# A convolution's norm moved in among the last steps of an attention, an SBUF copy issued sooner, and the second token tile split ahead of the last norm

## The reference, cut to what matters

```
for l in range(2):
    y = hybrid_mixer(x)                      # latent attention | convolution, then @ w_o
    x = layer_norm(ALPHA * x + y)            # "mix" norm
    y = memory_cross_attention(x, mem)       # @ w_q, softmax over 256 memory rows, @ w_o
    x = layer_norm(ALPHA * x + y)            # "cross" norm
    y = swiglu_ffn(x)                        # @ w_in, silu(g) * up, @ w_down
    x = layer_norm(ALPHA * x + y)            # "ffn" norm

def hybrid_mixer(x):
    c_q, c_kv, k_r, u = split(x @ w_in + b_in)
    y_att = mla_group(c_q, c_kv, k_r)        # 8 heads, 4 blocks of 128 queries, chunk-causal
    a, g = split(u)
    h = causal_depthwise_conv(a * sigmoid(g))            # 31 taps, 512 channels
    y_conv = silu(layer_norm(h) * cn_g + cn_b)           # norm over the 512 channels
    return concatenate([y_att, y_conv]) @ w_o
```

## Time and profile before

| what | value |
|---|---|
| median of 3 runs | 3571.17 us (3569.41 to 3573.1) |
| the profiled execution's own time | 3575.26 us |
| its span in the trace | 3573.4 us |
| PE busy | 3258.4 us (91%) |
| DVE busy | 1321.7 us (37%) |
| ACT busy | 875.4 us (24%) |
| mean granted TensorE clock | 0.954 of full speed |

### The profile page before, as it was taken

One profiled execution on the slowest core, in us unless ns is written; L12 is line 12 of the kernel. 1 busy time (PEld: TensorE's weight loads), 2 busy tenths in 40 slices (PEclk: granted clock), 3 DMA queues, 4 the chain that ended last, 5 costly groups with the idle time before them and its releaser, 6 DMA issues.

```text
span 3573.4 us, 35777 instructions
## 1 busy us (share of the span) xinstructions
PE 3258.4 (91%) x15128; PEld 2248.8 (63%) x15128; DVE 1321.7 (37%) x2223; ACT 875.4 (24%) x1387; POOL 131.4 (4%) x122
## 2 busy tenths in 40 slices
PE   6998899999998899998999999899699999999994
PEld 5677677877667677876888867677343333433331
DVE  3675443335675443335333444533311111111112
ACT  2342322222342322222233431122111111111111
POOL 0000000001000000001100000000100000000001
PEclk9999999999999999998999999899799999999997
DMA  4122122223112122322211321023599999999996
GB/s 153 59 71 83 59 83 92 97 98 117 59 62 92 59 83 92 103 102 85 74 54 54 94 75 53 33 92 143 209 425 426 426 425 426 426 425 426 426 426 240
DMA packets 229493, 627.62 MB, mean 176 GB/s; under 512 B 14736, under 2 KB 136464, under 8 KB 179920
## 3 DMA queue, kind: packets, MB, share of 16 engines
q1 hardware_dynamic: 207312, 579.37, 41.8%
q10 hardware_dynamic: 19824, 37.77, 3.0%
q0 software_dynamic: 2192, 8.13, 0.8%
HBM read 600.32 MB, written 22.81 MB: 174 GB/s over the span
## 4 chain that ended last, share of the span: by engine, by line
PE 66%; DMA 17%; DVE 10%; ACT 3%; POOL 2%; issue 2%; ACTq 0%; DVEq 0%; POOLq 0%
PE bank L120 64%; DMA piece<-in_moe_w 4%; DMA piece_high<-in_moe_w 3%; DMA mT_slot<-in_moe_w 3%; DMA xT<-in_moe_w 3%; DVE gate_acc L138 2%; PE bank L123 2%; DVE x_tok L138 1%; POOL root L135 1%; DMA memT<-in_moe_w 1%; DMA norm_room<-in_moe_w 1%; DMA y_att_slot<-in_moe_w 1%; DVE stat L153 1%; DVE piece_rounded L135 1%; ACT piece_high_rounded L126 1%
## 5 line engine op out<-in xcount | busy, mean ns | idle before, releaser
L120 PE MATMUL bank<-xT_rounded,piece_high_rounded 128*128 128x512 f32 (+1 forms) x1408 | 554.7, 394 | 25.1 <-DVE xT_low_rounded L135 25.1
L135 DVE TENSOR_TENSOR piece_rounded<-piece,piece_high_rounded 128x2048 fp32r<-128x2048 f32 (+1 forms) x156 | 342.1, 2199 | 575.2 <-ACT piece_high_rounded L126 574.8
L120 PE MATMUL bank<-xT_rounded,piece_rounded 128*128 128x512 f32 (+1 forms) x1408 | 542.1, 385 | 0.0
L120 PE MATMUL bank<-xT_low_rounded,piece_high_rounded 128*128 128x512 f32 (+1 forms) x1408 | 538.2, 382 | 0.0
L135 DVE TENSOR_TENSOR gate_and_hidden<-gate_and_hidden,bank 64x512 f32<-64x512 f32 x64 | 69.2, 1081 | 837.0 <-ACT gate_and_hidden L126 837.0
L126 ACT ACTIVATE piece_high_rounded<-piece 128x2048 fp32r<-128x2048 f32 (+1 forms) x156 | 283.0, 1820 | 287.6 <-DMA piece<-in_ffn_w_down 119.1
L120 PEld LDWEIGHTS bank<-xT_rounded,piece_high_rounded 128*128 128x128 f32 x1408 | 270.2, 192 | 80.9 <-DVE xT_low_rounded L135 26.3
L120 PEld LDWEIGHTS bank<-xT_low_rounded,piece_high_rounded 128*128 128x128 f32 x1408 | 269.9, 192 | 56.0 <-issue 4.4
L120 PEld LDWEIGHTS bank<-xT_rounded,piece_rounded 128*128 128x128 f32 x1408 | 268.4, 191 | 56.5
L120 PE MATMUL bank<-piece,xeT 128*64 128x512 f32 x488 | 239.1, 644 | 18.7 <-DMA piece<-in_moe_w 7.3
L120 PE MATMUL bank<-piece_high,xeT 128*64 128x512 f32 x464 | 185.3, 633 | 14.4 <-DMA piece<-in_moe_w 9.5
(11 more groups left out here) (337 smaller groups left out, 5054.3 us busy)
## 6 DMA issues: line engine op xcount, KB each, us to landing
piece<-in_moe_w SPq DMA_DIRECT2D x90, 1024.0 KB, 16.5
piece_high<-in_moe_w SPq DMA_DIRECT2D x88, 1024.0 KB, 16.5
xT<-in_moe_w SPq DMA_DIRECT2D x59, 1024.0 KB, 16.7
mT_slot<-in_moe_w SPq DMA_DIRECT2D x58, 1024.0 KB, 17.3
piece<-in_ffn_w_in SPq DMA_DIRECT2D x40, 1024.0 KB, 5.0
memT<-in_moe_w SPq DMA_DIRECT2D x30, 1024.0 KB, 15.8
y_att_slot<-in_moe_w SPq DMA_DIRECT2D x30, 1024.0 KB, 16.5
norm_room<-in_moe_w SPq DMA_DIRECT2D x29, 1024.0 KB, 17.0
```

What stands on the lines that cost most here:

```text
L120: return self.engine.matmul(*a, **k) if self.engine is not None else Nothing()
L135: return self.engine.tensor_tensor(*a, **k) if self.engine is not None else Nothing()
```

## The change

1. The convolution's norm. A new `z_turned_pe`, called in steps 28 to 31 of the attention's PE program behind the memory's keys, transposes tile i = n - 28. A new `z_dve`, called at the end of DVE's steps 29 to 32, norms tile n - 29. The result goes to a new tile `z_tok`, which lies where `mem_v_early` is, so `z_dve` also waits for the DMA that moves the memory's values away. `cross_pe` begins with the transposes back, ahead of the output product instead of between its first two groups.
2. That DMA is issued by ACT at the end of its step 23 instead of behind the attention.
3. In every output product with `turned`, tile 1 is transposed between the two pieces of tile 3 (`turned(1)`), and DVE splits tiles 0 and 1 both behind the norm of tile 2, ahead of the add and norm of tile 3. This is in the mix, cross and ffn products of both layers. The merge of the second network calls its `turned` at the old place alone.

```diff
@@ -326,6 +326,8 @@
         carve_from(XT_LOW_AT)
         y_room = carve("yT", CT, S, twin=True)
         self.mem_v_early = carve("mem_v_early", MT, D)
+        carve_from(XT_LOW_AT + CT * S)
+        self.z_tok = carve("z_tok", NT, CONV)
         carve_from(hT_at)
         z_room = carve("zT", CT, S, twin=True)
         self.yT = [y_room[:, k, :] for k in range(CT)] + [z_room[:, k, :] for k in range(CT)]
@@ -722,7 +724,7 @@
             e.also(key, "summed", half, i)
             self.banks.give((key, half, i), key, "added", half, i)
 
-    def project_out_pe(self, e, key, label, kt, lhs, lhs_ready, turned=None, behind_first=None):
+    def project_out_pe(self, e, key, label, kt, lhs, lhs_ready, turned=None):
 
         starts = list(range(0, kt, SLOT // BANK))
         for half in range(2):
@@ -733,8 +735,6 @@
                 for i in range(NT):
                     self.out_tile_pe(e, key, kt, lhs, lhs_ready, half, k0, n, i)
                 self.release(e, n)
-                if behind_first and not half and not k0:
-                    behind_first()
         if turned:
             n0, n1 = self.pe_piece(e, label), self.pe_piece(e, label)
             for tiles in ((0, 1), (2,), (3,)):
@@ -743,6 +743,8 @@
                         self.out_tile_pe(e, key, kt, lhs, lhs_ready, 1, k0, n, i)
                     if tiles[-1] == NT - 1:
                         self.release(e, n)
+                        if k0 == starts[-2]:
+                            turned(1)
                 if tiles == (2,):
                     turned(0)
 
@@ -1039,6 +1041,8 @@
                     self.half_values_pe(e, l, n)
                 else:
                     self.half_keys_pe(e, l, n - 16)
+                if h == HEADS - 1:
+                    self.z_turned_pe(e, l, i)
             if 2 <= n <= len(steps) + 1:
                 h, i = steps[n - 2]
                 bank = banks.take(e, "pT", l, n - 2)
@@ -1061,6 +1065,15 @@
                 ins.then_inc(*e.tick("pe", "y", l, n - 3))
                 if i == NT - 1 and h % 2 == 1:
                     banks.give(("y", l, h // 2), "y_split", l, h // 2)
+
+    def z_turned_pe(self, e, layer, i):
+
+        bank = self.banks.take(e, "zT", layer, i)
+        for c4 in range(CT):
+            e.wait_ge(*self.at("conv", layer, c4, TAPS - 1))
+        self.transposes(e, bank, [self.gate_acc[:, c4, i * P:(i + 1) * P] for c4 in range(CT)]).then_inc(
+            *e.tick("pe", "zT", layer, i))
+        self.banks.give(("zT", layer, i), "z", layer, i)
 
     def half_keys_pe(self, e, layer, u):
 
@@ -1205,6 +1218,11 @@
                     self.values_act(e, l, n // 4, n // 2 % 2)
                 else:
                     self.keys_act(e, l, n // 2 - 8)
+            if n == 23:
+                e.wait_ge(*at("pe", "k", l, HEADS // 2 - 1))
+                for q in range(4):
+                    e.wait_ge(*at("mem_v", l, q, MT - 1))
+                e.dma_start(self.mem_v, self.mem_v_early).then_inc(*e.lands("memory_values_moved", "mem_v_home", l))
 
     def mixer_dve(self, e, layer):
         l, at = layer, self.at
@@ -1282,7 +1300,22 @@
             if n < len(steps) and n % 4 == 0:
                 self.dve_piece(e, "memory values" if n < 16 else "memory keys")
             self.convolve(e, l, taps, 4)
-        self.taps = taps
+            if 0 <= n - len(steps) + 3 < NT:
+                self.z_dve(e, l, n - len(steps) + 3)
+        assert next(taps, None) is None
+
+    def z_dve(self, e, layer, i):
+        bank = self.bank("zT", layer, i)
+        e.wait_ge(*self.at("pe", "zT", layer, i))
+        e.bn_stats(self.stat[:, i, 0, :], bank[:, :]).then_inc(*e.tick())
+        e.wait_ge(*e.own())
+        e.bn_aggr(self.mean_var[:, i, :], self.stat[:, i, 0, :]).then_inc(*e.tick())
+        e.wait_ge(*e.own())
+        self.root_dve(e, i, 1, self.mean_var[:, i, 1:2], 1.0, LN_EPS, "z", layer, i)
+        e.wait_ge(*self.at("root", "z", layer, i))
+        e.wait_ge(*self.at("mem_v_home", layer))
+        e.tensor_scalar(self.z_tok[:, i, :], bank[:, :], self.mean_var[:, i, 0:1], self.root[:, i, 0:1],
+                        ALU.subtract, ALU.mult).then_inc(*e.tick("z", layer, i))
 
     def convolve(self, e, layer, taps, most):
         for _ in range(most):
@@ -1318,28 +1351,18 @@
     def cross_pe(self, e, layer):
         e.begin(f"cross{layer}")
         l, banks, at = layer, self.banks, self.at
-        for i in range(NT):
-            bank = banks.take(e, "zT", l, i)
-            for c4 in range(CT):
-                e.wait_ge(*at("conv", l, c4, TAPS - 1))
-            self.transposes(e, bank, [self.gate_acc[:, c4, i * P:(i + 1) * P] for c4 in range(CT)]).then_inc(
-                *e.tick("pe", "zT", l, i))
-            banks.give(("zT", l, i), "z", l, i)
-        def z_back():
-            for c4 in range(CT):
-                bank = banks.take(e, "zb", l, c4)
-                for i in range(NT):
-                    e.wait_ge(*at("z", l, i))
-                self.transposes(e, bank, [self.v_tok[:, i, c4 * P:(c4 + 1) * P] for i in range(NT)]).then_inc(
-                    *e.tick("pe", "zb", l, c4))
-                banks.give(("zb", l, c4), "silu", l, c4)
-
+        for c4 in range(CT):
+            bank = banks.take(e, "zb", l, c4)
+            for i in range(NT):
+                e.wait_ge(*at("z", l, i))
+            self.transposes(e, bank, [self.z_tok[:, i, c4 * P:(c4 + 1) * P] for i in range(NT)]).then_inc(
+                *e.tick("pe", "zb", l, c4))
+            banks.give(("zb", l, c4), "silu", l, c4)
         self.project_out_pe(e, f"mix{l}", "mix out", KD,
                             lambda k, i: (self.yT[k][:, i * P:(i + 1) * P], self.yT_low[k][:, i * P:(i + 1) * P]),
                             lambda k0: [("z_split" if k0 else "y_split", l, k) for k in range(CT)],
-                            lambda i: self.rows_to_T_pe(e, f"xT_mix{l}", i, self.x_tok, f"mix{l}", "normed", i), z_back)
-        for i in (1, 2):
-            self.rows_to_T_pe(e, f"xT_mix{l}", i, self.x_tok, f"mix{l}", "normed", i)
+                            lambda i: self.rows_to_T_pe(e, f"xT_mix{l}", i, self.x_tok, f"mix{l}", "normed", i))
+        self.rows_to_T_pe(e, f"xT_mix{l}", 2, self.x_tok, f"mix{l}", "normed", 2)
 
         for j in range(KD // 2):
             n = self.pe_piece(e, "cross query")
@@ -1397,8 +1420,7 @@
                             lambda k, i: (self.oT[:, k, i * P:(i + 1) * P], self.oT_low[:, k, i * P:(i + 1) * P]),
                             [("xo_split", l, h, v) for h in range(XH) for v in range(2)],
                             lambda i: self.rows_to_T_pe(e, f"xT_cross{l}", i, self.x_tok, f"cross{l}", "normed", i))
-        for i in (1, 2):
-            self.rows_to_T_pe(e, f"xT_cross{l}", i, self.x_tok, f"cross{l}", "normed", i)
+        self.rows_to_T_pe(e, f"xT_cross{l}", 2, self.x_tok, f"cross{l}", "normed", 2)
 
     def project_out_act(self, e, label, kt, begun=0):
         for _ in range(begun, 2 * len(range(0, kt, SLOT // BANK))):
@@ -1407,10 +1429,6 @@
     def cross_act(self, e, layer):
         e.begin(f"cross{layer}")
         l, at, a = layer, self.at, self.a
-        e.wait_ge(*at("pe", "k", l, HEADS // 2 - 1))
-        for q in range(4):
-            e.wait_ge(*at("mem_v", l, q, MT - 1))
-        e.dma_start(self.mem_v, self.mem_v_early).then_inc(*e.lands("memory_values_moved", "mem_v_home", l))
         self.act_piece(e, "mix out")
         for c4 in range(CT):
             low = self.yT_low[CT + c4]
@@ -1458,18 +1476,6 @@
     def cross_dve(self, e, layer):
         e.begin(f"cross{layer}")
         l, at = layer, self.at
-        self.convolve(e, l, self.taps, CT * TAPS)
-        for i in range(NT):
-            bank = self.bank("zT", l, i)
-            e.wait_ge(*at("pe", "zT", l, i))
-            e.bn_stats(self.stat[:, i, 0, :], bank[:, :]).then_inc(*e.tick())
-            e.wait_ge(*e.own())
-            e.bn_aggr(self.mean_var[:, i, :], self.stat[:, i, 0, :]).then_inc(*e.tick())
-            e.wait_ge(*e.own())
-            self.root_dve(e, i, 1, self.mean_var[:, i, 1:2], 1.0, LN_EPS, "z", l, i)
-            e.wait_ge(*at("root", "z", l, i))
-            e.tensor_scalar(self.v_tok[:, i, :], bank[:, :], self.mean_var[:, i, 0:1], self.root[:, i, 0:1],
-                            ALU.subtract, ALU.mult).then_inc(*e.tick("z", l, i))
         self.dve_piece(e, "mix out")
         for c4 in range(CT):
             low = self.yT_low[CT + c4]
@@ -1477,8 +1483,9 @@
             self.low_of(e, low, low, self.yT[CT + c4]).then_inc(*e.tick("z_split", l, c4))
         x_from = (lambda i: ("x_landed",)) if l == 0 else (lambda i: (f"ffn{l - 1}b", "normed", i))
         def turned(i):
-            if i >= 2:
-                self.rows_to_T_dve(e, f"xT_mix{l}", i - 2, self.xT, self.xT_low)
+            if i == 2:
+                for j in (0, 1):
+                    self.rows_to_T_dve(e, f"xT_mix{l}", j, self.xT, self.xT_low)
 
```

(14 more changed lines are left out.)

## The result

The changed kernel takes 3545.19 us, median of 4 runs (3544.39 to 3546.67); the kernel before, run beside it, 3572.14 (3569.41 to 3573.18, 4 runs). The ratio is 0.9926 with a 95% interval of 0.9909 to 0.9943: faster by 26.9 us, where 24.3 were forecast. Two repetitions beside the experiments gave 3545.57 (ratio 0.9929, 0.9915 to 0.9942) and 3543.45 (0.9925, 0.9911 to 0.9938). The profiled execution took 3544.39 us around a span of 3542.4, with a mean granted clock of 0.959; against the profile before, the spans differ by 31.0.

What follows compares the result with a forecast made beforehand. PE was taken to bound the kernel (busy 3258 of 3573 us), so only its waits pay. Norm -6.4, tails -19.1, ffn norms +1.2 and 0 sum to -24.3: from 3571.17 to 3546.9 us, range 3537 to 3558.

Steps and rivals of the forecast that it cites:

- The bank wait: Attention loop: PE waits 3.7 us ahead of step 30's keys for a bank released by DVE's first norm chain.
- The clock behind it: Attention loop: after the bank wait PE runs at its lower clock, losing 1.7 us, bounds 0 and 3.1.
- the chain: End of attention: from DVE's mask start at 259.5 to the last product, 6.8 us instead of 5.9.
- the forecast 266.3: Layer 0: the time in us at which the attention ends, 6.5 late.
- `z_split`: Mix out, layer 0: second group's operand ready at 276.1, where the group needs it at 279.1.
- The norm: Convolution's norm moved into the loop: mix out's second half starts 3.2 us earlier per layer, twice 6.4.
- The tails: Mix and cross outputs, both layers: queries gain 4.5, 5.6, 5.5 and 5.5, in all 21.1 us; 19.1 after clock deductions.
- the page of the Trainium skill: Clock falls only after gaps longer than the tails' waits and 2.26 us; by it tails give 21.1, total 3544.9.
- the 2.0: Mix and cross tails: deduction for clock dips, 0.5 us at each of four places, taking 21.1 to 19.1.
- The ffn norms: Behind the ffn norms: 1.2 us slower at layer 0, wait from 4.78 to about 6; layer 1 unchanged, 0.
- The DMA: Move of the memory's values issued near 228, taking 4.6 us, landing before 240, needed at 252; cost nothing.
- rival 3: Slower, through the DMA: `z_dve` waits for the move; landing after 264 decides, at 270 gives 3583 us; chance 0.03.

Runs made afterwards that it cites:

- Both cures: The two runs on the changed kernel that removed the bank wait: `e4_bank_later`, 3540.66 us, and `e3_norm_earlier`, 3538.13 us.
- `e3_norm_earlier`: Changed kernel with DVE's norm chains at steps 28, 29, 30 and 32 instead of 29 to 32; 3538.13 us, ratio 0.9913 to the kernel before.
- `e8_pe_order_old`: Changed kernel with tile 1's transposes on PE behind the last products again, DVE's new order kept; 3542.48 us, against 3545.57 for the changed kernel.
- `e4_bank_later`: Changed kernel with the banks of the forward transposes given back three steps later in PE's order; 3540.66 us, ratio 0.9915 to the kernel before.

## Why the prediction was right

**The bank wait** was forecast as 3.7 us ahead of the keys of step 30, and stands there with 3.10. It is shorter because PE arrives at 249.98 and not at the 249.17 taken: the transposes of steps 28 and 29 stand ahead of the wait too, and the loop as a whole ran 0.2 later in this execution, DVE with it. Both cures confirm what it is.

**The clock behind it** was the term with the widest bounds, 0 to 3.1, taken at 1.7. In layer 0 from the keys to the next scores it took 6.2 us (253.08 to 259.28) where `e3_norm_earlier` needs 3.4 (250.25 to 253.63): 2.8. Wait and clock together are 5.9 against 5.4 forecast. From DVE's mask to the last product the chain was forecast as 6.8 and measured as 6.8 (260.44 to 267.23), so the whole 0.9 us by which the attention ended later than the forecast 266.3 lay ahead of the mask. `z_split` was finished by 277.1 (forecast 276.1), 2.7 before its group. The norm gave 2.5 in layer 0 and 3.4 in layer 1, where 3.2 were forecast for each.

**The tails** were forecast at 21.1, less 0.5 for each for the clock. That deduction was mis-sized: no tail lost any clock. Behind waits of 1.17 and 1.49 the 256-column products started every 0.12 us, with a granted clock of 1.00 over 316 to 320. But the sum without it was too large too. The four gave 4.1, 5.2, 5.4 and 5.3, together 20.0, against 4.5, 5.6, 5.5 and 5.5. In layer 0's mix 0.3 of the missing 0.4 lie ahead of the query's first product, which comes 25.8 behind the start of the second half and not 25.5. So the two errors, 2.0 and 1.1, stand against each other. Here the page of the Trainium skill that the prediction set beside its sum (TensorE: Matmul & The Clock Gate, "HAM oscillation — how this bites in real kernels") was right: it lets short gaps pass without a lower clock. Taken as the prediction took it, for all gaps up to the 2.26 us ones, the trace still disagrees (below), and so does layer 1 of `e4_bank_later` behind 1.08 and 0.97.

**The total** is near the forecast partly by luck. Without the 2.0 the sum would have been -26.3, and the traces show just 26.3 up to the second network. But 1.6 of it is clock that the profiled execution before lost at one ffn place and the one after did not (next paragraph). Without that it is 24.7: 6.0 from the norm and 20.0 from the tails, less 1.3 at ffn 0. The medians differ by 26.9 in the first measurement and by 25.5 and 26.9 in the repetitions; where the 1 to 2 us beyond 24.7 come from isn't shown.

**The tail's two edits** were not told apart in the prediction, which took them as one. Its times came from DVE's queue alone, and `e8_pe_order_old` shows why that was enough: in mix and cross PE's part can be left out.

**The ffn norms.** The wait rose from 4.78 to 5.97 as forecast, and from tile 0's transposes to the latents it is 1.1 to 1.4 us longer. That the table shows 0.3 gained there is the clock: after the 2.26 us wait at 767.93 this execution lost none of it, where the one before lost about 1.6 at 779.94 (granted clock 1.00 over 768 to 774, and 0.72 over 779.9 to 785.9). At ffn 1 the forecast 0 was measured as 0.

**The DMA.** The move was issued at 227.24 and took 10.3 us and not 4.6, beside a weight piece issued at 226.87; in layer 1 it took 8.4. It landed at 237.5, and `z_tok` is first written at 252.22: rival 3, the slower side, needed a landing past 264 and was 26 us away from it. That the DMA would be hidden was right; its duration was taken from a row where it ran alone.

## What to carry to other kernels

Work moved into a loop that is short of PSUM banks is priced by where its bank is handed back, not by its engine time: walk the order of turns forward from each new hand-back until the same bank is taken again, and compare that with the releasing engine's queue. When a tail is slow, reorder the queue of the engine that feeds it before that of the engine that waits. Once an operand is ready early, let the waiting engine do what needs it instead of standing at the one item that isn't ready.

## What the runs showed of the hardware

**The clock after equal waits.** PE waits 2.26 us (or 2.25) ahead of the first ffn down product at four places in each trace. Two of them in the trace after:

```profile
583.19 0.77 PE L120 MATMUL bank<-piece_high_rounded,hidT_rounded 128*128 128x512 f32 x1 [2.26 <-DVE hidT_low_rounded L135]
583.75 0.63 PE L120 MATMUL bank<-piece_rounded,hidT_rounded 128*128 128x512 f32 x1
...
767.93 0.47 PE L120 MATMUL bank<-piece_high_rounded,hidT_rounded 128*128 128x512 f32 x1 [2.26 <-DVE hidT_low_rounded L135]
768.24 0.40 PE L120 MATMUL bank<-piece_rounded,hidT_rounded 128*128 128x512 f32 x1
```

At the first the next products take 0.63 and start every 0.43 us, 1.2 GHz; at the second they take 0.40 and start every 0.23, 2.4 GHz. The granted clock is 0.72 of full over 583 to 589 and 1.00 over 768 to 774:

```profile
583.00:589.00 6.00, 5.81 (x19) 4.72 (x20) 4.10 (x3) 2.61 (x2) 0.00 (x0) 0.72 0.29 113
...
768.00:774.00 6.00, 6.00 (x27) 4.96 (x28) 4.05 (x2) 2.71 (x2) 0.00 (x0) 1.00 0.69 277
```

Over the 13 traces of this study 38 of 52 such places were followed by about eight products at the lower clock (some 1.6 us lost), 14 by none, and the same place of one kernel fell on either side in different executions (583.19 above, and 582.24 in a repetition of the same kernel, where none was lost). The section of the Trainium skill named above has no lower clock after gaps of this length; the 38 disagree. The new 3.1 us wait shows the same spread: the eight keys behind it took from 1.99 to 3.78 us in different executions, 1.89 being full clock. A wait of 2 to 3 us therefore has an expected price and a spread of some 1.5 us each time, enough to hide an edit worth 1 us. Shorter waits were not always free either: `e4_bank_later` lost 1.5 us behind 1.08 and 0.97 in layer 1 and nothing behind the same two waits in layer 0, while none of the 44 tails with the new order, each with waits of 1.0 to 1.5, lost any. What in the execution decides it was not settled.

**One DMA, two durations.** The same 1 MB move inside SBUF took 4.6 us alone; beside a weight load of the same size it took 9.8 to 10.3 in layer 0 of the eleven traces with the early issue, and 8.3 to 8.6 in layer 1. What makes the two layers differ isn't shown.
